# Gathering a mixture-of-experts kernel's routed rows in quarter rows and transposing them on VectorE, with the blocks in a three-step pipeline

## The reference

```python
scores = sigmoid(x @ w_router);  # 64 experts in 8 groups, biased
idx = top_k(masked, 8)           # 8 experts for each token
w = scores[idx] / sum * ROUTED_SCALE
padded = ((counts + 127) // 128) * 128     # each expert's rows, in blocks of 128
...
(silu(xb @ w_exp_gate[e]) * (xb @ w_exp_up[e])) @ w_exp_down[e]   # per block
routed = segment_sum(y_assign * w, tok)
shared = (silu(x @ w_sh_gate) * (x @ w_sh_up)) @ w_sh_down        # all rows
```

## Time and profile before

| | us |
|---|---|
| median of 3 runs | 1980.0 |
| the runs | 1981.92, 1971.68, 1980.0 |
| the profiled execution's own time | 1980.55 |
| its span, first to last instruction | 1978.8 |

### The profile page before, as it was taken

The page is one execution under the profiler, slowest core; times in us unless marked ns, Lnnn a source line. Parts: engine busy times, 40 slices in busy tenths (PEclk is TensorE's granted clock), DMA queues, the critical chain, the costliest instruction groups (busy, mean ns, idle before and its releaser), DMA issues.

```text
span 1978.8 us, 29956 instructions
## 1 busy us (share of the span) xinstructions
PE 1756.0 (89%) x8454; PEld 1357.7 (69%) x8455; DVE 945.0 (48%) x1470; ACT 851.0 (43%) x952; POOL 774.8 (39%) x448
## 2 busy tenths in 40 slices
PE   4799999978889877789998999999999989999865
PEld 1667788868545555567777777888777767777642
DVE  5522310267466843245445455534554564445529
ACT  0521012421023431356557657634675676557623
POOL 2220000300100653256546547643564676646630
PEclk9799999987799888799999999999999999999988
DMA  9504531020552342369879989977899799879976
GB/s 330 171 19 163 173 105 35 14 86 1 194 208 91 98 174 65 113 223 343 249 234 356 299 259 355 323 197 216 265 334 286 255 363 327 292 204 345 343 227 275
DMA packets 104861, 425.84 MB, mean 215 GB/s; under 512 B 13244, under 2 KB 31801, under 8 KB 76656
## 3 DMA queue, kind: packets, MB, share of 16 engines
q1 hardware_dynamic: 62128, 279.38, 37.3%
q0 software_dynamic: 38800, 131.69, 25.6%
q10 hardware_dynamic: 3888, 14.16, 2.1%
HBM read 339.94 MB, written 85.25 MB: 215 GB/s over the span
## 4 chain that ended last, share of the span: by engine, by line
PE 51%; DMA 13%; DVE 12%; issue 9%; ACT 8%; another core or an unknown queue 3%; POOL 1%; ACTq 1%; DVEq 1%; SPq 0%; POOLq 0%
PE ps L792 22%; PE ps L1792 10%; DMA raw<-w_exp_up 7%; ACT gu_split L619 6%; PE ps L1923 5%; DMA arena<-hx_dram,arena 3%; PE ps L827 3%; PE ps L1740 3%; DVE gu_split L897 1%; DVE arena L1614 1%; DVE arena L1087 1%; PE ps L817 1%; DMA arena<-pos_sel 1%; PE ps L1765 1%
## 5 line engine op out<-in xcount | busy, mean ns | idle before, releaser
L792 PE MATMUL ps<-gu_split,xT 128*128 (+1 forms) x2736 | 664.3, 398 | 20.8 <-issue 20.6
L792 PEld LDWEIGHTS ps<-gu_split,xT 128*128 128x128 f32 x2736 | 511.9, 190 | 135.1 <-issue 31.6
L565 POOL TENSOR_TENSOR d_split<-raw,d_split (+1 forms) x65 | 303.8, 4674 | 248.8 <-ACT d_split L624 248.7
L792 PE MATMUL ps<-d_split,hTe 128*128 (+1 forms) x1356 | 335.4, 395 | 16.7 <-issue 12.0
L897 DVE TENSOR_TENSOR gu_split<-raw,gu_split (+1 forms) x130 | 292.6, 2292 | 87.1 <-ACT gu_split L619 80.2
L792 PEld LDWEIGHTS ps<-d_split,hTe 128*128 128x128 f32 x1356 | 258.8, 191 | 75.1 <-issue 16.8
L602 POOL DMA_INDIRECT acc_dram<-arena x104 | 202.9, 1951 | 163.5 <-ACT arena L717 143.5
L619 ACT ACTIVATE gu_split<-raw (+1 forms) x130 | 241.9, 1915 | 26.6 <-SPq L472 17.7
L1792 PE MATMUL ps<-hT_split,w_split 128*128 128x512 f32 (+1 forms) x816 | 192.5, 394 | 3.7 <-DVE w_split L1469 3.7
L1055 DVE TENSOR_TENSOR xT<-ps,xT 128x1024 fp32r<-128x1024 f32 x115 | 140.9, 1225 | 114.7 <-ACT xT L686 112.2
L1792 PEld LDWEIGHTS ps<-hT_split,w_split 128*128 128x128 f32 x816 | 152.1, 190 | 41.6 <-issue 6.0
(11 more groups left out here) (285 smaller groups left out, 1501.1 us busy)
## 6 DMA issues: line engine op xcount, KB each, us to landing
raw<-w_exp_gate SPq DMA_DIRECT2D x64, 1024.0 KB
raw<-w_exp_up SPq DMA_DIRECT2D x64, 1024.0 KB
raw<-w_exp_down SPq DMA_DIRECT2D x64, 1024.0 KB
arena<-w_ada SPq DMA_DIRECT2D x16, 1024.0 KB, 4.9
arena<-acc_dram SPq DMA_DIRECT2D x18, 512.0 KB, 18.2
arena<-w_ada SPq DMA_DIRECT2D x4, 2048.0 KB, 20.9
w_raw<-w_in SPq DMA_DIRECT2D x16, 512.0 KB, 4.8
acc_dram<-arena POOLq DMA_DIRECT2D x1, 5120.0 KB
```

Source lines behind the costliest of these rows:

```text
L565: tt(d_split(q, 1), raw_d(q), d_split(q, 0).bitcast(F32), ALU.subtract).then_inc(d_low, 1)
L792: last = mm(dst, lhs(a, j), rhs(b, j), start=(t == 0), stop=(t == len(terms) - 1))
```

## The change

- **Transposes of x go from PE to DVE.** `turn_x` is one DVE instruction that transposes within squares of 32x32: 128x1024, from `xg` to `xT_full`, a new name for the place of the low part of `xT`. It reads each partition's row with a step of 8 numbers. ACT makes the high part from `xT_full` (`x_high`), and DVE overwrites `xT_full` with the low part (`x_low`).
- **A square transposer can't move data between groups of 32 partitions, so the DMA does it.** `hx_dram` is seen as quarter rows of 256 numbers. Quarter r of 32 tokens goes to partitions 32r to 32r+31, and four indirect DMAs q = 0 to 3 take 32 tokens each, with index 4 x token + r. `lists` makes the table of indices `gtab` with 36 small products in place of four transposes, and DVE applies times 4, plus r (`quarter`). For the shared blocks `load_rows` does the same with four DMAs.
- **Padding rows are not gathered.** The four gathers have `bounds_check=4*T-1, oob_is_err=False`: an index of a padding row is out of bounds and nothing is moved. The trash rows of `hx_dram` are gone. The scatter is as before.
- **Down's low part goes from POOL to DVE** (`down_low`), at the end of DVE's step.
- **Three steps.** PE's step is gate and up of block b; transpose h of block b-1; down of block b-2. y has two pairs of PSUM banks (`y_banks`) in place of one; the two banks of x's transposes are free for them. The steps of the other engines follow; after the loop come one transpose of h and two downs.
- **`routed_steps`**: the first pair is written out, since its `scatter` and `routed_out` belong to shared blocks; the loop starts with the second. The end is computed on the device as an even number of blocks.
- **h2 isn't permuted** when it is written; `transpose_h2` reads it with a step of 8 numbers.
- The products, their order and count in a block, the weights' loads, and the split of gate and up are as they were.

```diff
-            def gather(b, p, j):
-                pool.indirect_dma_start(out=xg[:, p, :], out_offset=None, in_=hx_dram, in_offset=...(ap=gidx[:, p:p + 1]...
+            quarters = hx_dram.rearrange("t (b x) -> (t b) x", b=4)
+            def gather(b, p, j):
                 pool.wait_ge(gidx_ready, j + 1)
                 pool.wait_ge(x_t, b - 1)
+                for q in range(4):
+                    pool.sem_inc(dma_turns)
+                    pool.indirect_dma_start(out=xg[:, p, q * 256:(q + 1) * 256], out_offset=None, in_=quarters, in_offset=bass.
+                                            IndirectOffsetOnAxis(ap=gidx[:, p, q:q + 1], axis=0),
+                                            bounds_check=4 * T - 1, oob_is_err=False).then_inc(xg_in[p], 16)
+            def step(s, p, j):                                # POOL
+                gather(s + 4, p, j + 4)
+                if not (isinstance(j, int) and j < 2):
+                    scatter(s - 2, p, j - 2)

+            def step(b, p, j):                                # ACT
+                silu(b, p)
+                h_high(b - 1, 1 - p)
+                x_high(b + 2, p)
+                if_new(act, j + 2, gate_up_high)
+                ...                                           # routed_out(b - 2, p, j - 2)
+                if_new(act, j, down_high)

-                for c in range(KD):
-                    last = pe.transpose(ps[:, c // 4, ...], xg[:, p, c * P:(c + 1) * P], ident)
-                last.then_inc(x_t, 1)
+            def step(b, p, j):                                # PE
+                gate_up(b, p, j)
+                turn_h(b - 1, 1 - p)
+                down(b - 2, p, j - 2)

+            def turn_x(b, p, j):
+                ...                                           # wait for the four quarters
+                dve.transpose(xT_full[:, p, 1, :].rearrange("p (c q j) -> p q c j", c=KD, q=4),
+                              xg[:, p, :].rearrange("p (q i c) -> p q c i", q=4, c=KD)).then_inc(x_t, 1)
+            def down_low(nx):                                 # was POOL's
+                q = nx % 2 if isinstance(nx, int) else dve.snap(nx % 2)
+                dve.wait_ge(d_high, nx + 1)
+                tt(d_split(q, 1), raw_d(q), d_split(q, 0).bitcast(F32), ALU.subtract).then_inc(d_low, 1)
+            def step(b, p, j):                                # DVE
+                gate(b, p)
+                turn_x(b + 2, p, j + 2)
+                h_low(b - 1, 1 - p)
+                x_low(b + 2, p)
+                next_gather(p, j + 4)
+                if_new(dve, j + 2, gate_up_low)
+                if not (isinstance(j, int) and j < 2):
+                    next_scatter(p, j - 2)
+                if_new(dve, j, down_low)

-                stt(h2[:, i % 2, :].rearrange("p (j q) -> p q j", j=KD), perm(y), scale, perm(sh2_row[:, c, :]),
+                stt(h2[:, i % 2, :], y, scale, sh2_row[:, c, :], ALU.mult, ALU.add).then_inc(h2_ready, 1)
```

More of the change, by code:

```diff
@@ L432, in routed_steps @@
         def routed_steps(eng, step):
+            for j in range(2):
+                step(NT + j, (NT + j) % 2, j)
             total = routed_blocks(eng)
-            with eng.Fori(0, PAIRS) as i:
+            with eng.Fori(1, PAIRS) as i:
                 with eng.If(2 * i < total):
@@ L688, in step @@
+            for b in range(2):
+                x_high(b, b)
+                load_rows(b + 2)
+                if b == 0:
                     ln_std(2 * NT - 2, x1[:, (NT - 1) % 2, :])
                     logits_out(NT - 2)
[L690 to L696 removed]
@@ L731, in phase3_act @@
+            for b in range(NT):
+                shared_step(b, b % 2)
+            last = routed_steps(act, step)
+            h_high(NT + last + 1, (NT + 1) % 2)
+            for u in range(2):
+                routed_out(NT + last + u, (NT + u) % 2, last + u)
             act.wait_ge(moe_done, 1)
@@ L855, in phase3_pe, with gate_up @@
-            for b in range(-2, NT):
-                step(b, b % 2, b - NT)
-                if is_block(b, -1):
-                    rank(1)
-                if is_block(b, 0):
-                    route(NT - 1)
-                if is_block(b, 2):
+            def gate_up(b, p, j):
+                x, q = expert(j)
+                pe.wait_ge(xT_ready, b + 1)
+                pe.wait_ge(gu_low, x + 1)
+                w = [gu_split(q, s).rearrange("p (t c n) -> p t c n", t=2, c=KD) for s in range(2)]
+                products(ps[:, 2 + p, :].rearrange("p (t n) -> p t n", t=2),
+                         lambda s, c: xT[:, p, s, c * P:(c + 1) * P], lambda s, c: w[s][:, :, c, :], KD).then_inc(gu_mm, 1)
@@ new lines, in turn_h, with down @@
+            def turn_h(b, p):
+                pe.wait_ge(h_ready, b + 1)
+                at_least(pe, hT_ready, b)
+                for c in range(2):
+                    last = pe.transpose(ps[:, 6, c * P:(c + 1) * P], h_sb[:, p, c * P:(c + 1) * P], ident)
+                last.then_inc(ht_mm, 1)
+            def down(b, p, j):
+                x, q = expert(j)
+                pe.wait_ge(hT_ready, b + 1)
+                at_least(pe, y_ready, b - 1)
+                pe.wait_ge(d_low, x + 1)
+                v = [d_split(q, s).rearrange("p (c n) -> p c n", c=2) for s in range(2)]
+                for h in range(2):
+                    last = products(ps[:, y_banks(p), :][:, h, :], lambda s, c: hTe[:, p, s, c * P:(c + 1) * P],
+                                    lambda s, c: v[s][:, c, h * 512:(h + 1) * 512], 2)
+                last.then_inc(y_mm, 1)
@@ L875, in phase3_pe @@
                     mm(ps[0:1, 7, 4 * E:4 * E + NBP], ones[0:E, :], cmp_b, start=True, stop=True).then_inc(blk_mm, 1)
-            routed_steps(pe, step)
+            last = routed_steps(pe, step)
+            turn_h(NT + last + 1, (NT + 1) % 2)
+            for u in range(2):
+                down(NT + last + u, (NT + u) % 2, last + u)
             for i in range(NT):
@@ new lines, in next_gather, with next_scatter @@
+            def next_gather(p, j):
+                dve.tensor_copy(gidx[:, p, :], gtab[:, bass.ds(j, 1), :].rearrange("p o q -> p (o q)")).then_inc(gidx_ready, 1)
+            def next_scatter(p, j):
+                dve.wait_ge(y_out[p], landed_before(j, p))
+                dve.tensor_copy(sidx[:, p:p + 1], tok_t[:, bass.ds(j, 1)]).then_inc(sidx_ready, 1)
+            for b in range(2):
+                turn_x(b, b, b - NT)
+                x_low(b, b)
+                if b == 0:
+                    x1_norm(NT - 1)
+                else:
+                    h2_norm(NT - 1)
@@ new lines, in step @@
+            def step(b, p, j):
+                gate(b, p)
+                turn_x(b + 2, p, j + 2)
+                h_low(b - 1, 1 - p)
+                x_low(b + 2, p)
+                next_gather(p, j + 4)
[3 more added lines that the diff above has]
+                if_new(dve, j, down_low)
+            for b in range(NT):
+                shared_step(b, b % 2)
+                if b == 0:
@@ L1112, in phase3_dve @@
                     dve.wait_ge(tables_ready, 1)
-            routed_steps(dve, step)
+            last = routed_steps(dve, step)
+            h_low(NT + last + 1, (NT + 1) % 2)
+            for u in range(2):
+                next_scatter((NT + u) % 2, last + u)
             dve.wait_ge(ln2_in, 48)
```

333 lines of the change are left out of this document (166 added, 167 removed).

## The result

The changed kernel takes 2036.56 us (median of 4 runs, 2031.34 to 2041.98) against 1979.46 for the kernel before: ratio 1.0296, 95% interval 1.0255 to 1.0336. It is slower by 57 us. The forecast was 2010, with a range of 1942 to 2032. The profiled execution took 2031.34 us, its span 2029.6.

The account below looks back on a forecast made before the run. The prediction took PE, with DMA also near its limit, to bound the routed stage and the bound to move to VectorE: 1980.6 + 44 (stage) - 9 (start) - 3 (end) = 2012, say 2010 us, range 1942 to 2032.

Parts of the forecast that it names:

- the forecast's own: Whole kernel: the main forecast of 2010 us, without the rivals, ranged from 1990 to 2035; its chance was 0.47.
- VectorE's step: Routed stage: VectorE's in-order list takes 13.1 us with a new expert, 5.3 without; stage 1076 us before late gathers.
- the end: After the last gate/up: 8.4 + 0.3 us instead of 11.8, so 3 us faster.
- Transposes off PE: Routed blocks on PE: 0.90 us of each goes, 9.31 to 8.41; worth 167 us if PE stayed the bound.
- The turn: VectorE's added 128x1024 transposition per block: taken as 2.0 us, lower end 1.25.
- the first rival: Turn on VectorE costs 1.25 us, a read with a step being free; 1960 us, faster; chance 0.36.
- the one for waits: Routed stage: late gathers stall VectorE in its list; 10 us, between 0 and 25.
- The start: Start of the routed stage: removed waits outweigh added list products and later gathers; 9 us faster, between -20 and +8.
- that chain: Stage start, lists to first routed product: gather issues, landing, two turns, two low parts; 16 to 18 us, 7 to 9 uncovered.
- POOL: GpSimd's five issues a block in place of two: 7.0 us by medians, under 8.41, so hidden.
- the second rival: POOL becomes the bound if a gather averages 1.6 us; step 9.85 us, time 2040 us; chance 0.07.
- The third: Rival: DMA was the true bound and PE's relief changes nothing; 1970 us; chance 0.10.

Follow-up runs that it names:

- the probe: Changed kernel with the turn reading its quarter rows without a step (output in another order): 1959.59 us, ratio 1.0056.
- the run with whole rows: Changed kernel with one gather of whole 4 KB rows per block in place of four of 1 KB: 2025.02 us, ratio 1.0243.

## Why the prediction was wrong

The direction and the main mechanism were right: the bound moved from PE to VectorE, and the time freed on PE in the stage made nothing shorter. The time came out 5 us past the range, and 2 us past the forecast's own of 1990 to 2035. Two terms failed: the waits in VectorE's step, and the end.

- **Transposes off PE.** As forecast, none of it counts. PE's busy time in the stage fell by 39 us and not by 92 (102 x 0.90), since the products behind many of the waits ran at a lower granted clock (0.64 to 0.80 in the 30 slow blocks, for 0.99 over the old stage); PE didn't set the pace, so that cost nothing more.
- **The turn.** Taken 2.0, measured 2.11 (2.12 median); the first rival's 1.25 would have held only for a read without a step (1.23). The rows with a step on the write side were good neighbours, though misread: 1.07 us for 512 elements and 2.00 for 1024 are 2.1 and 2.0 ns an element, not 1.7, and the rows without a step have 1.2 to 1.35. The 0.11 us too little is some 8 us of the stage, an estimate by the probe's 68 us for 0.89. The Trainium skill's rule on 16-byte lines ("SBUF — State Buffer", "Door 1: The DMA port swizzle") agrees with the reads here: 0.89 us more for 1024 reads 32 bytes apart. That no such price lies on the write in runs of 32 numbers agrees with it too.
- **VectorE's step.** 13.1 us forecast with both splits, 12.65 measured, since in the timeline most instructions start 0.1 us before the one ahead of them has ended. But the splits of gate and up (block j+2) and of down (block j) meet in only 38 of the 103 steps; 25 steps have the first alone (median 10.46), 25 the second alone (9.07), 15 none (6.57). I had put both in one step and 5.3 us in the next. The sum over the medians is 480.7 + 261.5 + 226.8 + 98.6 = 1068 us, near what I had (1076 for 104), but that is partly luck: by my own terms these four kinds of step would be 13.1, 10.8, 7.6 and 5.3 us, together 1037.
- **The failing term of the stage is the one for waits.** I put 10 us, between 0 and 25, for late gathers, and waits for ScalarE only at the copy of x and at gate and up. Gate to gate the 103 steps sum to 1106 us. The list of waits above names what is in them. Late gathers are 22.7 us in seven steps, more than the 10 but within its bounds; they lie in most of the longest steps, for example 3.85 us in the step of 16.7 us at 1788. 7.5 of the 22.7 are the first gather behind the wait for the shared blocks, which I had not followed in GpSimd's queue. What the sum put at nothing is VectorE's wait for ScalarE's high part of down, 50.8 us in 25 steps, and before the gate 26.6 us in 16. The first makes the steps with down's split alone 9.07 us long and not 7.6: ScalarE's copy of x, its copy of y and the high part of down stand in a row behind the turn, and VectorE's low part waits for the last of them, as in this step:

```profile
1091.72 2.12 DVE L1122 STREAM_TRANSPOSE xT_full<-arena 128x1024 f32<-128x1024 f32 x1
...
1093.88 1.06 ACT L696 ACTIVATE xT<-xT_full 128x1024 fp32r<-128x1024 f32 x1 [4.63 <-DVE xT_full L1122]
1094.85 1.10 ACT L718 ACTIVATE arena<-ps,arena 128x1024 f32<-128x1024 f32 x1
...
1095.84 1.90 ACT L639 ACTIVATE d_split<-raw  x1
...
1098.10 2.29 DVE L1114 TENSOR_TENSOR d_split<-raw,d_split  x1 [1.76 <-ACT d_split L639]
```

- **The start** gave 21 us where 9 were forecast. 17 of them are PE's busy time (118.9 to 101.9 us): its transposes of x took 13.1 us there where I counted 4, and its products 7.0 us less than before (336 for 348, at a granted clock of 0.84 for 0.81). PE's idle time fell only from 44.3 to 40.3 us: the waits of 8.43 and 4.27 us are gone, and one of 12.05 us ahead of the first routed product has come. My 16 to 18 us for that chain add up to some 20.
- **The end is the second failing term, +13.3 for -3, and it misses by as much as the stage (+59.3 for +44).** I counted PE's products alone. The loop's 16 empty turns stand between the last routed step and the work behind the loop (PE idle 10.15 us), and beside it runs a chain that I had not written down: scatter of block 101 in the step of block 103, its landing, copy of y of block 103, last scatter. With the empty turns alone taken away the end is 105.1 us; with the scatter first as well it was 100.7, which is still 6 more than before. The scatter's place was not tried alone, so how much of the 13 each of the two has stays open. In the kernel before a scatter was issued in its own block's step, and nothing of the routed blocks stood behind the loop.
- **POOL.** 7.0 us a block forecast by the median issue. The median was right (1.04), but the mean of an issue was 1.46: beside VectorE's subtractions of two SBUF operands it takes 1.78 us. The prediction put the long issues of the earlier trace rows, up to 3.0 and 3.5 us, down to a full DMA; in the trace of the kernel before they are those beside L897, which has two SBUF operands too (scatters 2.89 us on the mean beside it and 1.59 elsewhere). GpSimd still was not the bound, as the run with whole rows shows, so the second rival falls, though its 2040 us lies nearest to the result: that is a coincidence. The third falls with the plain read, since the stage changed by 68 us with the DMA's work unchanged.

## What to carry to other kernels

Work moved to an engine that has spare time costs what its list costs in order, waits for its partner engine included: write both engines' lists out for every class of step, at the distance at which each part of it occurs, before adding a long instruction. When the order of a pipeline is changed, follow the last blocks through every queue to the end, empty loop turns and landings included. Try the parts of a change one by one, and together: here the order costs 1.8% by itself, gains with one small move beside it (1.2% together, with the gate moved as well), and the large move that came with them turns this into a loss of 3%.

## What the runs showed of the hardware

- A transposition of squares on VectorE, 128x1024 in float32, takes 1.23 us with a plain read and 2.12 us with reads 32 bytes apart; writes in runs of 128 bytes cost nothing (1.23 us with them and without).
- A subtraction on VectorE with both operands in SBUF and one on GpSimd exclude each other (1.23 us becomes 4.88 us on the mean of 37, 6.84 in the row shown); with one operand in PSUM VectorE's stays at 1.23 us.
- An indirect gather's issue on GpSimd takes 1.00 us on the mean (178 issues, at most 1.04), and 1.78 us (254 issues, up to 3.1) where such a subtraction of VectorE (L960, L1114, L1128) overlaps it. Beside the turn it stays at 1.00 us (109 issues that begin within one). From the changed kernel:

```profile
1600.05 1.00 POOL L596 DMA_INDIRECT arena<-hx_dram,small  x1 [0.30 <-issue]
...
1605.58 2.45 POOL L596 DMA_INDIRECT arena<-hx_dram,small  x1 [0.30 <-issue]
1608.34 1.86 POOL L596 DMA_INDIRECT arena<-hx_dram,small  x1 [0.30 <-issue]
```

The first lies beside the turn at 1599.28, the others beside L960 at 1604.83.
